# A decoder layer with a streamed mixture of experts: banks of the first gather, a reordered routing, weight transfers of 4 MB, and a last item in halves

## What the reference computes

```python
def moe(h, w_r, b_r, w_gu, b_gu, w_dn, b_dn):
    ht = h.reshape(n * t, d)                       # 264 x 1024
    logits = ht @ w_r + b_r                        # 32 experts
    top_val, top_idx = lax.top_k(logits, 4)
    gate = softmax(top_val)                        # spread into dense_gate (264 x 32)
    for e in range(32):
        gu = ht @ w_gu[e] + b_gu[e]                # 1024 x 2048: gate and up columns
        x_glu = minimum(gu[:, :1024], 7.0)
        x_lin = clip(gu[:, 1024:], -7.0, 7.0)
        act = x_glu * sigmoid(1.702 * x_glu) * (x_lin + 1.0)
        out = out + dense_gate[:, e:e+1] * (act @ w_dn[e] + b_dn[e])   # 1024 x 1024
```

## Time and profile before

| | |
|---|---|
| time, median of 3 runs | 1281.93 us (1281.57 to 1285.98) |
| the profiled execution, its own time | 1282.66 us |
| its span, first to last instruction | 1280.9 us |
| TensorE busy | 1249.9 us (98%) |
| VectorE, ScalarE, GpSimd busy | 442.8, 216.7, 27.7 us |
| granted TensorE clock, mean | 0.996 of 2.4 GHz |
| moved by DMA | 470.35 MB |

### The profile page before, as it was taken

One profiled execution on the slowest core, in us unless ns is written; L12 is line 12 of the kernel. 1 busy time (PEld: TensorE's weight loads), 2 busy tenths in 40 slices (PEclk: granted clock), 3 DMA queues, 4 the chain that ended last, 5 costly groups with the idle time before them and its releaser, 6 DMA issues.

```text
span 1280.9 us, 17088 instructions
## 1 busy us (share of the span) xinstructions
PE 1249.9 (98%) x6479; PEld 597.9 (47%) x6479; DVE 442.8 (35%) x1267; ACT 216.7 (17%) x443; POOL 27.7 (2%) x74
## 2 busy tenths in 40 slices
PE   9999999999999999999999999999999999999897
PEld 7879856876743333433333343333333333333332
DVE  5759893273322222332222332222223322222222
ACT  3341334211311111111111111111111111111112
POOL 4000020000000000000000000000000000000000
PEclk9999999999999999999999999999999999999999
DMA  9421648599989999999999999999999999999993
GB/s 315 162 98 33 230 134 338 188 382 378 392 326 424 428 426 425 427 428 428 426 428 428 429 428 429 428 428 429 429 427 429 429 428 428 429 428 427 428 427 162
DMA packets 55658, 470.35 MB, mean 367 GB/s; under 512 B 7100, under 2 KB 7485, under 8 KB 27565
## 3 DMA queue, kind: packets, MB, share of 16 engines
q1 hardware_dynamic: 51406, 458.71, 86.5%
q0 software_dynamic: 2560, 9.80, 2.0%
q10 hardware_dynamic: 1647, 1.19, 0.4%
HBM read 463.97 MB, written 6.29 MB: 367 GB/s over the span
## 4 chain that ended last, share of the span: by engine, by line
PE 80%; DMA 16%; DVE 2%; ACT 1%; issue 1%; SPq 0%; POOL 0%; DVEq 0%; ACTq 0%; POOLq 0%
PE banks L1154 44%; PE banks L666 13%; DMA region_m<-in_w_gu 8%; DMA ring<-in_w_gu 8%; PE banks L1238 5%; PE banks L965 4%; PE banks L1204 2%; PE banks L1221 2%; PE banks L1216 1%; PE banks L851 1%; PE banks L731 1%; PE banks L859 1%; PE banks L1063 1%; PE banks L1090 1%; DVE region_p L1955 1%; PE banks L1042 1%
## 5 line engine op out<-in xcount | busy, mean ns | idle before, releaser
L1154 PE MATMUL banks<-ring,region_p 128*64 128x512 f32 x2208 | 489.6, 595 | 10.6 <-DMA ring<-in_w_gu 10.5
L1154 PEld LDWEIGHTS banks<-ring,region_p 128*64 128x64 f32 x2208 | 153.4, 137 | 329.6 <-issue 296.8
L2275 DVE TENSOR_SCALAR region_p<-banks 128x512 f32<-128x512 f32 x32 | 22.1, 692 | 663.5 <-PE banks L1154 663.5
L1154 PE MATMUL banks<-region_m,region_p 128*64 128x512 f32 x736 | 166.3, 600 | 4.8 <-DMA region_m<-in_w_gu 4.8
L666 PE MATMUL banks<-hT,ring 128*128 128x264 f32 x512 | 117.7, 387 | 0.4 <-ACT ring L1523 0.4
L1154 PEld LDWEIGHTS banks<-region_m,region_p 128*64 128x64 f32 x736 | 51.3, 138 | 112.3 <-issue 100.7
L666 PEld LDWEIGHTS banks<-hT,ring 128*128 128x128 f32 x512 | 95.7, 190 | 16.8 <-ACT ring L1523 0.8
L2238 DVE TENSOR_TENSOR xT<-xT,banks 128x264 f32<-128x264 f32 x248 | 89.5, 423 | 0.7
L1238 PE MATMUL banks<-region_p 64*128 64x264 f32 x496 | 82.1, 415 | 0.0
L1687 ACT COPY region_p<-banks 128x264 f32<-128x264 f32 x33 | 12.5, 379 | 355.8 <-PE banks L1216 355.8
L1238 PEld LDWEIGHTS banks<-region_p 64*128 64x128 f32 x496 | 52.0, 185 | 34.7 <-issue 30.3
(11 more groups left out here) (416 smaller groups left out, 918.7 us busy)
## 6 DMA issues: line engine op xcount, KB each, us to landing
ring<-in_w_gu SPq DMA_DIRECT2D x92, 2048.0 KB, 26.6
ring<-in_w_dn SPq DMA_DIRECT2D x46, 2048.0 KB, 29.5
region_m<-in_w_gu SPq DMA_DIRECT2D x30, 2048.0 KB, 27.3
region_m<-in_w_dn SPq DMA_DIRECT2D x16, 2048.0 KB, 30.9
ring<-in_w_in SPq DMA_DIRECT2D x5, 2048.0 KB, 13.8
ring<-in_cache_mem_k SPq DMA_DIRECT2D x7, 1024.0 KB, 17.2
late<-in_w_gu SPq DMA_DIRECT2D x6, 1024.0 KB, 13.2
ring<-in_cache_mem_v SPq DMA_DIRECT2D x5, 1024.0 KB, 9.5
```

What stands on the lines that cost most here:

```text
L1154: ins = pe.matmul(bank[n][u * SLOTS:(u + 1) * SLOTS, :], lhs, rhs, start=start, stop=stop)
L2275: dve.tensor_scalar(xg, bank[0][:, :], 7.0, None, ALU.min).then_inc(sem("glu_clipped"), 1)
```

## The change

- `first_banks`: the first gather uses the banks of the jobs `h_tok` 4, 5, 0 and 1 (banks 1, 2, 3, 4) for its two gathers and its two turns, in place of banks 0 to 3. The remaining banks (0, 5, 6, 7) are waited for behind the first turn.
- Routing: `hT` of the last chunk is made by DVE right behind the last `xo` addition, not by ACT; the first part of the norm's sums goes from between the logits' chunks to the head of the `moe_norm` job; ACT takes the roots of all three token groups in one Ln and one Exp, in place of two of each; DVE's negated maxima go from before the match to behind the mask.
- Weights: in memory order each partition now gets four rows of `w_gu` (32 KB together) for two pieces, or eight rows of `w_dn`. `piece_src` takes half of that (16 KB, at a pitch of 32 KB). `pair_src` takes all of it: in the loop SP issues one transfer of 4 MB for two pieces, waits until both slots have been used, and TensorE waits for the even piece alone.
- `FIRST_QUADS` goes from 2 to 3, and SP now writes out the last quad too, in pieces of 2 MB; so the 4 MB transfers serve quads 3 to 6 of 0 to 7, 48 transfers for 96 pieces.
- Columns: `line_halves` gives each 64-partition half of banks 0 and 1 the columns that lie in one half of each run of eight fp32 (four columns, then four skipped), in place of one half of the row. The biases of gate and up are read the same way. `h_tok` is stored with a factor of 4 in place of 2 x 2.
- Last item: the fourth gate and up piece arrives in two transfers of 1 MB with a wait each; the activations are made, turned and copied in two halves (`activate_last`, `turn_half`), and the down product runs over both pieces for each half (`second_weights_half`). ACT's load of the Ln and Exp table goes behind the two copies.

```diff
+        first_banks = [job(("h_tok", i)) % 8 for i in (4, 5, 0, 1)]
...
         def piece_src(e, s):
             if s < 4:
-                return w_gu[0, e, 2 * s * P:2 * (s + 1) * P, :].rearrange("(p v) n -> p (v n)", v=2)
-            return w_dn[0, e, 4 * (s - 4) * P:4 * (s - 3) * P, :].rearrange("(p v) n -> p (v n)", v=4)
+                rows = w_gu[0, e, 512 * (s // 2):512 * (s // 2 + 1), :]
+                return rows.rearrange("(p r v) n -> p r (v n)", r=2, v=2)[:, s % 2, :]
+            return w_dn[0, e].rearrange("(p r v) n -> p r (v n)", r=2, v=4)[:, s - 4, :]
+
+        def pair_src(e, s):
+
+            if s == 4:
+                return w_dn[0, e].rearrange("(p v) n -> p (v n)", v=8)
+            return w_gu[0, e, 256 * s:256 * (s + 2), :].rearrange("(p v) n -> p (v n)", v=4)
...
-        FIRST_QUADS = 2
+        FIRST_QUADS = 3
+
+        LAST_GU = PIECES * UNROLL - 3
...
-            with sp.Fori(FIRST_QUADS, nq) as q:
+            with sp.Fori(FIRST_QUADS, lq) as q:
                 e0 = (q * UNROLL) % E
-                for n in range(PIECES * UNROLL):
-                    sp.wait_ge(sem("piece_used"), PIECES * UNROLL * q + (n - NSLOT + 1))
-                    sp.dma_start(piece_slot(n % NSLOT), piece_src(e0 + n // PIECES, n % PIECES)).then_inc(
+                for n in range(0, PIECES * UNROLL, 2):
+                    sp.wait_ge(sem("piece_used"), PIECES * UNROLL * q + (n - NSLOT + 2))
+                    sp.dma_start(pair_slots(n % NSLOT), pair_src(e0 + n // PIECES, n % PIECES)).then_inc(
                         sem(f"piece{n % NSLOT}"), 16)
+            for n in range(PIECES * UNROLL):
+                sp.wait_ge(sem("piece_used"), PIECES * UNROLL * before_last + (PIECES * UNROLL + n - NSLOT + 1))
+                dst, src = piece_slot(n % NSLOT), piece_src(E - UNROLL + n // PIECES, n % PIECES)
+                if n == LAST_GU:
+                    for h in range(2):
+                        sp.dma_start(dst[:, 2 * h * D:2 * (h + 1) * D], src[:, 2 * h * D:2 * (h + 1) * D]).then_inc(
+                            sem("last_half" if h else f"piece{n % NSLOT}"), 16)
+                else:
+                    sp.dma_start(dst, src).then_inc(sem(f"piece{n % NSLOT}"), 16)
...
                 elif kind == "moe_norm":
+                    open_bank(pe, key)
+                    pe.wait_ge(sem("x3_sum"), 2)
+                    last_token_sums(key, x3_sq_long, 0)
                     pe.wait_ge(sem("x3_sq"), KT)
                     last_token_sums(key, x3_sq_long, 1)
                 elif kind == "logits":
...
                     def chunk_ready(k):
+
                         if k == KT - 1:
-                            open_bank(pe, ("moe_norm",))
                             pe.wait_ge(sem("x3_sum"), 1)
-                            last_token_sums(("moe_norm",), x3_sq_long, 0)
-                        pe.wait_ge(sem("h_moe"), k + 1)
+                        else:
+                            pe.wait_ge(sem("h_moe"), k + 1)
...
                 for c in range(2):
-                    bank_free(c)
+                    bank_free(first_banks[c])
...
+            def line_halves(w):
+
+                w = w.rearrange("p (q e v) -> p e q v", e=2, v=4)
+                return w[:, 0], w[:, 1]
...
                     for g in range(2):
-                        ins = halves(g, x_k, w[:, g * D:g * D + 512], w[:, g * D + 512:(g + 1) * D],
+                        ins = halves(g, x_k, *line_halves(w[:, g * D:(g + 1) * D]),
                                      s == 0 and v == 0, s == 3 and v == 1)
...
             pe.wait_ge(sem("act_ready"), last + 1)
-            turn(act_rows, 4, "act_turned")
+            turn_half(0, 4)
             scatter_rows(1, False)
-            pe.wait_ge(sem("glu_clipped"), last + 1)
-            pe.wait_ge(sem("gu_read"), last + 2)
+
+            pe.wait_ge(sem("act_ready"), last + 2)
+            turn_half(1, 1)
+
+            pe.wait_ge(sem("glu_clipped"), last + 2)
             residual_sample()
             scatter_sample(False)
-            second_weights(last_quad, u, False, (4,))
+            second_weights_half(0)
             turn_gates(last + 1, 4)
-            second_weights(last_quad, u, False, (5,))
+            second_weights_half(1)
...
+            def activate_last(i):
...
+                clip_gate(0)
+                line(0)
+                clip_gate(1)
+                product(0).then_inc(sem("act_ready"), 1)
+                line(1)
+                product(1).then_inc(sem("act_ready"), 1)
```

More of the change, by code:

```diff
@@ L1217, in turn_gates @@
                 ins.then_inc(sem("scat_t"), 1)
+            def line_halves(w):
+                w = w.rearrange("p (q e v) -> p e q v", e=2, v=4)
+                return w[:, 0], w[:, 1]
             def add_bias(n, r, start):
-                for u in range(2):
-                    pe.matmul(bank[n][u * SLOTS:(u + 1) * SLOTS, :], one_hot[r * E:(r + 1) * E, :],
-                                    bias_sb[r * E:(r + 1) * E, u * 512:(u + 1) * 512], start=start, stop=False)
+                b = bias_sb[r * E:(r + 1) * E, :]
+                for u, rhs in enumerate((b[:, 0:512], b[:, 512:D]) if r == 2 else line_halves(b)):
+                    pe.matmul(bank[n][u * SLOTS:(u + 1) * SLOTS, :], one_hot[r * E:(r + 1) * E, :], rhs, start=start,
+                              stop=False)
             def scatter(i, part):
@@ L1243, in _ @@
             first_turn()
-            for n in range(4, 8):
-                bank_free(n)
+            for n in range(8):
+                if n not in first_banks:
+                    bank_free(n)
             def place_free(i):
@@ L1253, in rows_in, with wait_piece @@
                 pe.wait_ge(sem("hg_ready"), i + 3)
-            def wait_piece(q, u, first, s):
+            def wait_piece(q, u, where, s):
                 n = PIECES * u + s
-                if first:
+                if where == "first":
                     n += PIECES * UNROLL * q
@@ L1262, in wait_piece, with weights @@
                     j = n % NSLOT
-                    pe.wait_ge(sem(f"piece{j}"), landed(q, n))
-                return j
-            def weights(q, u, first, s):
-                j = wait_piece(q, u, first, s)
+                    if where == "last":
+                        pe.wait_ge(sem(f"piece{j}"), landed_last(q, n))
+                    elif s % 2 == 0:
+                        pe.wait_ge(sem(f"piece{j}"), landed(q, n))
+                return j
+            def weights(q, u, where, s):
+                j = wait_piece(q, u, where, s)
+                n = PIECES * u + s
                 for v in range(2):
+                    if where == "last" and n == LAST_GU and v == 1:
+                        pe.wait_ge(sem("last_half"), 16)
                     x_k = hg[:, 2 * (s % 2) + v, (s // 2) * SLOTS:(s // 2 + 1) * SLOTS]
@@ L1282, in biases, with second_weights @@
                 add_bias(1, 1, False)
-            def second_weights(q, u, first, pieces=(4, 5)):
+            def second_weights(q, u, where, pieces=(4, 5)):
                 pe.wait_ge(sem("act_t_ready"), UNROLL * q + u + 1)
                 for s in pieces:
-                    j = wait_piece(q, u, first, s)
+                    j = wait_piece(q, u, where, s)
                     for v in range(4):
@@ L1292, in second_weights, with item @@
                     ins.then_inc(sem("piece_used"), 1)
-            def item(q, u, first):
+            def item(q, u, where):
                 i = UNROLL * q + u
                 place_free(i)
-                if first and q == 0 and u == 0:
+                if where == "first" and q == 0 and u == 0:
                     pe.wait_ge(sem("hg_ready"), 2)
@@ L1300, in item @@
                     rows_in(i)
-                weights(q, u, first, 0)
-                if first and q == 0 and u == 0:
+                weights(q, u, where, 0)
+                if where == "first" and q == 0 and u == 0:
                     rows_in(0)
@@ L1305, in item @@
                 for s in range(1, 3):
-                    weights(q, u, first, s)
+                    weights(q, u, where, s)
                 turn_gates(i)
                 biases(i)
-                weights(q, u, first, 3)
+                weights(q, u, where, 3)
                 gather(i + 1)
@@ L1315, in item @@
                 scatter(i, 1)
-                second_weights(q, u, first)
+                second_weights(q, u, where)
             for q in range(FIRST_QUADS):
                 for u in range(UNROLL):
-                    item(q, u, True)
+                    item(q, u, "first")
             pe.wait_ge(sem("routed"), 3)
@@ L1324, in _ @@
                 for u in range(UNROLL):
-                    item(q, u, False)
+                    item(q, u, "loop")
             for u in range(UNROLL - 1):
-                item(last_quad, u, False)
+                item(last_quad, u, "last")
             u = UNROLL - 1
@@ L1727, in _ @@
             scatter_matrix(last, 4)
```

(10 more changed lines are left out.)

97 lines of the change are left out of this document (70 added, 27 removed).

## The result

The changed kernel took **1273.87 us** (median of 4 runs, 1273.79 to 1275.33) against 1282.51 us (4 runs) for the kernel before: ratio 0.9924, 95% interval 0.9909 to 0.9939. Run once more, beside the last three experiments, it took 1274.81 us (6 runs, 1273.53 to 1278.36) against 1283.04: 0.9938, 0.9923 to 0.9954. The profiled span fell from 1280.9 to 1272.1 us, by 8.8.

What follows compares the result with a forecast made beforehand. The DMA weight stream sets the time from about 880 us, TensorE before it. Start -4.7, transfers -3.6, code +0.3, last quad -1.7, halves -0.6 make -10.3 off 1282.66, less 0.7 for the median: 1271.6 us, range 1268 to 1278.5.

Steps and rivals of the forecast that it cites:

- part 3: Weight stream in the loop: 4 MB transfers save a fixed cost of 0.076 us each, -3.6 us over 48 pairs.
- Part 1: First gather: new banks avoid the count wait and half clock, sample passes overlap the selection; first weights 4.4 us sooner.
- part 6: Last item: activations, turn and down product in halves start the down product sooner, -0.6 us.
- Part 2: Routing ahead of the first gather: one Ln and Exp fewer, maxima moved behind the mask, -0.3 us.
- part 5: Last quad: TensorE arrives level or late, so its long wait and the half clock after it go, -1.7 us.
- part 4: Third quad written out: about 5 more instruction packets, each delaying a DMA engine, +0.3 us, bounds 0 and +1.2.
- rivals B: First gather's gain is eaten, by a clock that still falls or a lagging DMA engine: 1273.5 us, chance 0.07.
- C: Last item waits for its last piece, so the last-quad and halves gains give nothing: 1273.9 us, chance 0.05.
- Rival A: Weight stream: 4 MB transfers gain nothing, since the cost is per 16 KB run: 1275.2 us, chance 0.17.
- Part 7: Strided column reads of banks 0 and 1 in 72 passes per item: no cost, 0 us.
- Rivals D: TensorE reads strided columns slower and becomes the bound in all items; near 1750 us at half-clock rate, chance 0.04.
- E: First quads and last: 16 KB pieces at 32 KB pitch stream slower; 1327 us at 383 GB/s, chance 0.03.

Runs made afterwards that it cites:

- e9: The changed kernel run again without any edit, beside the kernel before: 1274.81 us, ratio 0.9938.
- e6: The changed kernel with the first gather back in banks 0 to 3: 1279.16 us, ratio 0.9963.
- e1: The kernel before with only the new banks of the first gather: 1280.22 us, ratio 0.9967.
- e5: The changed kernel with the old routing order (two Ln and two Exp, last hT chunk by ACT, maxima ahead of the match): 1276.49 us, ratio 0.9940.
- e3: The changed kernel with the old memory order, each 4 MB transfer made of two 16 KB runs per partition, columns unstrided: 1279.30 us, ratio 0.9960.
- e2: The changed kernel with every pair in the loop issued and waited for as two 2 MB pieces: 1280.73 us, ratio 0.9967.
- e7: The changed kernel with two first quads written out in place of three, so 60 pairs in all: 1275.96 us, ratio 0.9945.
- e11: The changed kernel with four first quads written out in place of three, so 12 pairs fewer: 1278.23 us, ratio 0.9963.
- e10: The changed kernel with each 4 MB transfer cut into two of 64 partitions, runs still 32 KB: 210 GB/s, against 431 with 128 partitions.

## Why the prediction came out as it did

Predicted 1271.6 us, measured 1273.87, inside the range of 1268.0 to 1278.5, on the predicted side. An earlier start of the stream, a faster stream and a shorter end all came as forecast, but the number owes something to luck: part 3 had the right size from a wrong mechanism, and the overlaps counted in parts 1 and 6 did not come in full. The sum (-10.3) was 1.5 too large against the profiles (-8.8): 0.6 because the stage ahead happened to run later, 0.6 in parts 1 and 2, 0.4 in part 5 and 0.3 in part 6, less 0.4 in part 4. Another 0.6 lies in the kernel before, whose median was 1281.93 over three runs and 1282.51 over four. The time alone can't tell the forecast from rivals B (1273.5) and C (1273.9), which lie nearer to it; the profile can. The gather ran at full clock, and the last piece came in time.

- **Part 1, banks (-4.4).** 3.85 us. The step that failed is the overlap: "the 8 passes of the sample tokens run while DVE still selects". They could not, for TensorE was busy with the position products until 349.92, when VectorE was selecting too, so all 24 passes of the gather (2.96 us) lie behind that and not 16. By the prediction's own 0.107 us a pass the 8 are 0.86 us; the part came out 0.55 short. That no half clock comes in the gather was right, for all 12 kernels profiled with the new banks (2.96 us). But in 8 of the 12 (the rows of the table with 4.24 or 4.45) the clock falls ahead of it, in the turning of `h_tok`, which then takes up to 1.66 us more. The bank edit can't be the cause, since that turning is over before the first instruction that the edit touches. The two profiles with the old banks did not have it, which is too few to tell. What sets off the fall was not isolated: the engine's timeline of e9 has no idle time of note from 341.3 us on.
- **The start moves the end one for one.** Shown by e6 (918.5 against 918.2 from the first weights on) and e1.
- **Part 2, routing (-0.3).** 0.26 less at full clock, 0.13 to 0.23 more at half clock (e5).
- **Part 3, 4 MB transfers (-3.6).** Measured 3.6, but for another reason. The step that failed is "a fixed cost per transfer": e3 has the transfers of 4 MB without the long runs and gains nothing, so the price of 0.076 us is per 128 runs. That the size was right is luck. 1 MB pieces to 2 MB pieces, and 2 MB pieces to pairs, both halve the number of runs, so the extrapolation held all the same; that the price of the first step is of the same kind is inferred from its equal size (0.076 and 0.075 us), not tried. Rival A had the cost right (per run) and the run's length wrong: 32 KB goes as one packet. That the order of memory was changed, and not only the size of the transfer, is what paid.
- **Part 4, code (+0.3).** About -0.1 for two things that nearly cancel. With a third quad written out one more landing ahead of 760 us is late, by 1.3 to 1.5 us, above the bound of 1.2: the eight pieces up to 756.8 us took 40.6 us in e2, 39.2 up to 755.1 us in before. Ahead of the last quad, instruction packets come in up to 799 us in e2 and up to 683 in before. Against that, one landing of the last quad came late in the kernels with two quads written out (5.99 us behind the one before it in before, 6.39 in e1, 6.30 in e7) and in e11 with four (6.44), while with three it was 5.07 at most. An instruction packet lies in the queue in 1212 to 1217 us of before. That such a packet holds one DMA engine back, and that a landing waits for that engine, was read from its place in time, not tried.
- **Part 5, last quad (-1.7).** 1.28, since TensorE comes to the last item's fourth piece 0.88 us behind its landing, not 0.5. I put the end of the half clock down to TensorE arriving later because of the pairs, and that is one of two ways. With neither pairs nor a third quad written out TensorE waited 2.34 us (before) and 2.74 (e1) and got half clock. With pairs alone (e7) the landing was late too, by 6.30 us, but TensorE arrived later, waited 1.08 and kept the clock. With the third quad alone (e2) the late landing is missing, the wait was 1.26, and the clock stayed. After has both, and TensorE does not wait there at all, so either would have done.
- **Part 6, halves (-0.6).** 0.33. VectorE came out as drawn (products ended 2.3 and 3.7 us in, 2.3 and 3.8 predicted). The step that failed is "only a short turn (0.45) and the sample's residual and scatter (1.1) stand behind the second", for it leaves out what stands ahead of it. The residual passes and the first turn run to 1251.4, the scatter of 1.13 us behind them to 1252.4, and only then, 4.2 us in and not 3.8, comes the second turn. From 1248.1 on TensorE has no idle time before the down product, so a still faster VectorE would gain nothing there. The last two pieces landed in time (1248.52 and 1253.52, used at 1253.92 and about 1255.6), so rival C did not come.
- **Part 7, strided columns (0).** 0: an item takes TensorE 27.74 us before and after, and the same in e3. Rivals D and E are out: 428 GB/s in the first quads, with 16 KB at a pitch of 32 KB. The Trainium skill's rule on 16-byte lines that are hit at least twice (SBUF — State Buffer, "Door 1: The DMA port swizzle") agrees with this. Rival D's price was read too high: the earlier trace rows gives 1.7 us more for 16 passes at half clock, 0.11 a pass and not 0.21.
- **The range and the chances.** By the prediction's own terms the lower end is 1269.4 us (1281.93 - 12.5), not 1268, and rival C (1273.9) lies below 1275.5, so it belonged to "faster". Neither changes how the result is read.

## What to carry to other kernels

When a stream of transfers sets the time, look for what the price hangs on before enlarging the transfer: compare two kernels that have the same transfers but different contiguous runs, and count packets on the page. A step that starts the stream sooner is worth its full length at the end, but pairs of slots may only be asked for once the queue is deep enough to survive the wait for two. And look at more than one execution before a clock is put into a sum: the same code turned the same six banks in 2.78 us in one and in 4.24 in the next.

## What was not expected of the hardware

- A run of 32 KB per partition counts as one packet and saves 9.4 ns per packet saved and DMA engine; 48 transfers fewer of the same runs save nothing (e3 against e2).
- Transfers of 64 partitions, one behind the other in the queue, run at 210 GB/s, those of 128 at 431 (e10).
- The same code took 1.5 to 1.7 us longer at half clock in the turning of `h_tok` (345 to 352 us) in some executions and not in others, with no idle time ahead of it, and about 2 us more between 140 us and the router's product (clock 0.91 in 140 to 160 us).
- Waits of 2.34 and 2.74 us were followed by 16 passes of 5.35 us, waits of 1.08 to 1.26 us by 3.65.
